# A decoder layer on one core: the decode step's delta rule with four heads on the partitions, its state products in column groups, and a new written-out order

## What is computed

```python
def gated_delta_rule(q, k, v, log_a, beta, s0):     # decode: one chunk of c = 4 tokens per sequence
    g = jnp.cumsum(log_a, axis=-1)
    decay = jnp.where(lower, jnp.exp(jnp.where(lower, diff, 0.0)), 0.0)     # diff = g_i - g_j
    kk = jnp.einsum("bhnid,bhnjd->bhnij", k, k)
    a_mat = eye + jnp.where(strict, beta[..., :, None] * kk * decay, 0.0)
    rhs = jnp.concatenate([v * beta[..., None], k * (beta * jnp.exp(g))[..., None]], axis=-1)
    sol = lax.linalg.triangular_solve(a_mat, rhs, left_side=True, lower=True, unit_diagonal=True)
    u, w = sol[..., :dv], sol[..., dv:]
    qk = jnp.einsum("bhnid,bhnjd->bhnij", q, k) * decay
    v_new = u_c - jnp.einsum("bhcd,bhde->bhce", w_c, s)
    o_c = (jnp.einsum("bhcd,bhde->bhce", q_c * jnp.exp(g_c)[..., None], s)
           + jnp.einsum("bhij,bhje->bhie", qk_c, v_new))
    s = (s * jnp.exp(g_last)[..., None]
         + jnp.einsum("bhcd,bhce->bhde", k_c * jnp.exp(g_last - g_c)[..., None], v_new))
```

## Time and profile before

| | us |
|---|---|
| runs | 1472.62, 1476.36, 1477.51 (median 1476.36) |
| the profiled execution's own time | 1477.91 |
| its span | 1476.1 |
| TensorE busy in the span | 1447.0 (98%) |
| VectorE, ScalarE, GpSimd busy | 712.0, 477.5, 204.0 |
| mean granted clock of TensorE | 0.988 |

### The profile page before, as it was taken

One profiled execution on the slowest core, in us unless ns is written; L12 is line 12 of the kernel. 1 busy time (PEld: TensorE's weight loads), 2 busy tenths in 40 slices (PEclk: granted clock), 3 DMA queues, 4 the chain that ended last, 5 costly groups with the idle time before them and its releaser, 6 DMA issues.

```text
span 1476.1 us, 25520 instructions
## 1 busy us (share of the span) xinstructions
PE 1447.0 (98%) x9772; PEld 1414.6 (96%) x9772; DVE 712.0 (48%) x1303; ACT 477.5 (32%) x876; POOL 204.0 (14%) x262
## 2 busy tenths in 40 slices
PE   7999999999999999999999999999999999999997
PEld 7899998999999899999999999999999999999997
DVE  5678844677663635433333333333333333344625
ACT  6324451442424424432130221302213022145525
POOL 3100213142243432000000000000000000140303
PEclk9999997999999999999999999999999999999999
DMA  7112421412223442211111111111111111112003
GB/s 181 44 44 58 101 77 30 131 59 65 80 77 77 96 88 56 55 46 44 43 44 55 45 43 43 43 53 48 43 43 44 50 51 43 43 43 73 30 29 118
DMA packets 166318, 89.88 MB, mean 61 GB/s; under 512 B 50763, under 2 KB 160267, under 8 KB 166230
## 3 DMA queue, kind: packets, MB, share of 16 engines
q1 hardware_dynamic: 165222, 84.89, 20.9%
q0 software_dynamic: 1008, 3.79, 0.6%
HBM read 77.97 MB, written 10.69 MB: 60 GB/s over the span
## 4 chain that ended last, share of the span: by engine, by line
PE 63%; DVE 2%; issue 1%; ACT 0%; DMA 0%; DVEq 0%; POOL 0%; SPq 0%
PE pg L712 62%; DVE act_lo L2040 1%; PE bk L1167 0%; DMA out<-y_tok 0%; DVE y_tok L2124 0%; PE bk L1097 0%; ACT act_hi L1186 0%; DVE xres L2164 0%; DVE tm L2161 0%; ACT sq L1186 0%; PE bk L1112 0%; ACT L1186 0%; DVE xres L2049 0%; PE bk L1158 0%; DVE tm L2150 0%
## 5 line engine op out<-in xcount | busy, mean ns | idle before, releaser
L712 PE MATMUL pg<-act_hi,w_hi 128*128 128x352 f32 x1320 | 428.9, 325 | 8.3 <-issue 3.7
L712 PE MATMUL pg<-act_lo,w_hi 128*128 128x352 f32 x1320 | 424.7, 322 | 0.0
L712 PE MATMUL pg<-act_hi,w_lo 128*128 128x352 f32 x1296 | 416.8, 322 | 0.0
L712 PEld LDWEIGHTS pg<-act_hi,w_hi 128*128 128x128 f32 x1320 | 249.0, 189 | 11.4 <-issue 5.9
L712 PEld LDWEIGHTS pg<-act_lo,w_hi 128*128 128x128 f32 x1320 | 249.5, 189 | 0.0
L712 PE MATMUL pg<-u_hi,w_hi 128*128 128x352 f32 x768 | 249.3, 325 | 0.0
L712 PE MATMUL pg<-u_hi,w_lo 128*128 128x352 f32 x768 | 248.9, 324 | 0.0
L712 PE MATMUL pg<-u_lo,w_hi 128*128 128x352 f32 x768 | 247.8, 323 | 0.0
L712 PEld LDWEIGHTS pg<-act_hi,w_lo 128*128 128x128 f32 x1296 | 244.1, 188 | 0.0
L1186 ACT ACTIVATE w_hi<-w_raw 128x1024 fp32r<-128x1024 f32 x111 | 117.0, 1054 | 354.5 <-PE pg L712 322.0
L2387 POOL TENSOR_TENSOR ssq<-ssq,sq 128x352 f32<-128x352 f32 x72 | 76.1, 1065 | 876.4 <-ACT sq L1186 875.5
(11 more groups left out here) (341 smaller groups left out, 1527.0 us busy)
## 6 DMA issues: line engine op xcount, KB each, us to landing
w_raw<-in_w_up SPq DMA_DIRECT2D x32, 512.0 KB, 4.0
w_raw<-in_w_down SPq DMA_DIRECT2D x32, 512.0 KB, 3.4
w_raw<-in_w_in SPq DMA_DIRECT2D x29, 512.0 KB, 3.8
x_tok<-in_x_prompt SPq DMA_DIRECT2D x8, 512.0 KB, 7.7
w_raw<-in_w_out SPq DMA_DIRECT2D x8, 512.0 KB, 4.3
x_col<-in_x_prompt SPq DMA_DIRECT2D x32, 128.0 KB, 2.7
w_raw<-in_w_ple_gate SPq DMA_DIRECT2D x8, 512.0 KB, 3.9
out<-y_tok SPq DMA_DIRECT2D x8, 512.0 KB, 3.0
```

What stands on the lines that cost most here:

```text
L712: last = mm(pg[bank][:, 0:TH], w, a, start=i == 0, stop=i == len(terms) - 1)
```

## The change

All four heads of the decode batch go on the partitions beside each other: the 4 x 32 = 128 (head, token) pairs are the rows of one 128x128 matrix, whose blocks off the diagonal are masked away (`m_smp`, `m_lev` are now 128x128, `m_bat` is 128x8, made from `m_row`). So each step is one product where it was four.

- `s_norm` also makes `q_col` (log decay, beta and the last factor as columns of 128 rows) by three products with one moving column; `s_begin` prepares them.
- `s_xt` is now a block transpose on VectorE and no step of TensorE; `s_turn` is gone; `s_kk` turns k and v.
- `s_in`: the k (steps 0, 1) and q (steps 2, 3) of a sequence, scaled and placed so that all other tokens are zero (`placed()`, in `pre[1]`, which GpSimd clears first), are 32 columns of weights, and the state is the moving operand with 128 columns. The products of the four heads go to four column groups (output partitions 0, 32, 64, 96) and accumulate over the 8 sequences. 64 products in all, 16 per step.
- `s_out` adds the q part by a product with the identity.
- `s_put 0` and `s_put 1`: four products each, one per head, with 32 rows (head h on rows 32h to 32h+31), 128 columns of weights and 512 moving columns, into four banks. GpSimd makes two copies of 128x512 instead of eight of 32x512. All four decays on VectorE come before the first add.
- The states are written out after the adds of `s_put 1`.
- `ORDER` is new for the whole mixer. The 1464 fills are the same; the new list has 157 steps, 89 of them with no fill behind them, the old one 168 and 69.

```diff
@@ ORDER, the stretch of the decode step @@
-z 0 6 25; kq 1 0 15; s_wait 0 0 10;
-s_begin 0 0 13; s_conv 0 0 14; s_norm 0 0 21; s_conv 1 0 7; s_kk 0 0 7; s_conv 2 0 10; s_xt 0 0 2; s_in 0 0 4;
-s_in 1 0 4; s_y 0 0 2; s_in 2 0 4; s_in 3 0 3; s_z 0 0 2; s_in 4 0 4; s_in 5 0 4; s_in 6 0 4; s_in 7 0 4;
-s_turn 0 0 7; s_solve 0 0 10; s_out 0 0 14; s_onorm 0 0 0; s_put 0 0 0; s_put 1 0 11; s_put 2 0 0;
-s_put 3 0 14; s_put 4 0 0; s_put 5 0 23; s_put 6 0 0; s_put 7 0 52; diff 2 0 0; vturn 0 0 0; vturn 1 0 0;
-diff 3 0 18; kk 2 0 0; into 0 0 0; kk 3 0 6; kturn 0 0 2; solve 0 0 15; b1 2 0 0; b2 2 0 67; b3 2 0 0;
+z 0 6 75; kq 1 0 0; s_wait 0 0 0;
+s_begin 0 0 0; s_conv 0 0 44; s_norm 0 0 1; s_conv 1 0 30; s_kk 0 0 0; s_conv 2 0 8; s_in 0 0 3; s_xt 0 0 0;
+s_in 1 0 2; s_y 0 0 8; s_in 2 0 3; s_in 3 0 2; s_z 0 0 4; s_solve 0 0 12; s_out 0 0 13; s_onorm 0 0 0;
+s_put 0 0 27; s_put 1 0 67; vturn 0 0 0; diff 2 0 0; vturn 1 0 0; diff 3 0 30; kk 2 0 0; into 0 0 0; kk 3 0 0;
+kturn 0 0 17; solve 0 0 19; b1 2 0 20; update 0 0 0; sum 0 0 0; b2 2 0 11; b3 2 0 60; b4 2 0 5; into 1 0 0;
...
@@ names @@
+        QSQ, QN, YC, GAM = [LY[0][:, i, :] for i in range(4)]
+        KSQ, KN, PTB, OSQ = [LY[1][:, i, :] for i in range(4)]
+        DEC, AMAT, LOWB, XTB = [AT[1][:, i, :] for i in range(4)]
+        VT, U, KT, WV = [XT1[0][:, i, :] for i in range(4)]
+        PUT_BANKS = (bk[0], bk[2], bk[3], bk[4])
+        PUT = (AT[0], X[0])
+        def zone(b, i):
+            return bk[b][:, P * i:P * i + P]
+        def by_head():
+            return pre[1][:, PAD:PAD + TP].rearrange("p (h i m) -> p h i m", h=H, m=TS)
+        def placed():
+            pitch = pre[1][:, :].ap[0][0]
+            return bass.AP(pre[1], PAD, [[pitch, P], [TS * NB, H], [TS + NT, NB], [1, NT]])
@@ SyncE @@
-                        sp.wait_ge(sm.s_out_made, 2 * (h + 1))
+                        sp.wait_ge(sm.s_out_made, H + h + 1)
@@ TensorE @@
-            def against_state(g):
-                for i in range(4 * g, 4 * g + 4):
-                    last = mm(bk[4][:, 8 * i:8 * i + 8], S_in[:, i // NB, i % NB, :], F0[:, 8 * i:8 * i + 8], start=True, stop=True)
+            def against_state(c, i0):
+                for i in range(i0, i0 + NB // 2):
+                    for h in range(H):
+                        last = mm(zone(4, c)[quad(h)], by_head()[:, h, i, :], S_in[:, h, i, :], start=i % NB == 0, stop=i == NB - 1)
...
                 elif k == "s_norm":
+                    for j in range(3):
+                        last = mm(bk[3][:, j:j + 1], X0[:, j, :], ones[0:TS, 0:1], start=True, stop=True)
...
                 elif k == "s_kk":
+                    mm(zone(0, 1), KN, KN, start=True, stop=True)
+                    mm(zone(0, 2), KN, QN, start=True, stop=True)
+                    turn(zone(3, 0), KN, ident[:, :])
+                    turn(zone(3, 1), WV, ident[:, :]).then_inc(sm.q_pe, 1)
...
                 elif k == "s_in":
-                    last = against_state(c)
+                    elif c == 2:
+                        pe.wait_ge(sm.q_dve, 12)
+                    last = against_state(c // 2, c % 2 * (NB // 2))
...
+                elif k == "s_out":
+                    mm(zone(1, 0), WV, PTB, start=True, stop=False)
+                    mm(zone(1, 0), QSQ, ident[:, :], start=False, stop=True).then_inc(sm.q_pe, 1)
...
                 elif k == "s_put":
-                    if c >= 4:
-                        pe.wait_ge(sm.s_out_made, c - 3)
-                    mm(bk[c % 4][:, :], F0[0:TS, c // 2 * P:(c // 2 + 1) * P], by_seq[c % 4][0:TS, :, :],
-                       start=True, stop=True).then_inc(sm.q_pe, 1)
+                    pe.wait_ge(sm.q_pool, 6 + c)
+                    if c == 0:
+                        pe.wait_ge(sm.q_act, 13)
+                        pe.wait_ge(sm.q_dve, 14)
+                    else:
+                        pe.wait_ge(sm.s_out_made, H)
                     for h in range(H):
+                        last = mm(PUT_BANKS[h][:, :], KT[quad(h)], PUT[c][quad(h), :, :], start=True, stop=True)
@@ VectorE @@
+                elif k == "s_xt":
+                    dve.wait_ge(sm.q_pool, 5)
+                    nc.vector.transpose(XB, XTB).then_inc(sm.q_dve, 1)
...
                 elif k == "s_put":
-                    dve.wait_ge(sm.q_pe, 10 + c)
-                    dve.wait_ge(sm.q_dve, 13 + c // 2)
-                    part = S_in[:, c // 2, 4 * (c % 2):4 * (c % 2) + 4, :]
-                    tt(part, part, heads(bk[c % 4]), ADD).then_inc(sm.s_out_made, 1)
+                    dve.wait_ge(sm.q_pe, 9 + c)
+                    dve.wait_ge(sm.q_dve, 18)
+                    dve.wait_ge(sm.states_out, 16 * 6)
+                    for h in range(H):
+                        now = S_in[:, h, 4 * c:4 * c + 4, :]
+                        tt(now, now, heads(PUT_BANKS[h]), ADD).then_inc(sm.s_out_made, 1)
@@ GpSimd @@
                 elif k == "s_begin":
+                    nc.gpsimd.memset(pre[1][:, PAD:PAD + TP], 0.0).then_inc(sm.q_pool, 1)
...
+                elif k == "s_out":
+                    for i in range(2):
+                        tt(PUT[i][:, :, :], WV[:, None, :].to_broadcast([P, 4, P]), spread(m_bat[:, 4 * i:4 * i + 4], P), MUL) \
+                            .then_inc(sm.q_pool, 1)
```

More of the change, by code:

```diff
@@ L66 @@
[L66 to L74, removed]
+begin 0 0 0; diff 0 0 8; diff 1 0 1; kk 0 0 90; kk 1 0 21; b1 0 0 3; b2 0 0 72; b3 0 0 9; b4 0 0 58; y 0 4 0;
@@ new lines @@
+y 2 4 0; y 3 4 0; norm 0 0 0; z 2 4 0; z 3 4 0; kturn 1 0 12; y 2 5 0; kq 2 0 0; solve 1 0 10; update 1 0 0;
+z 2 5 0; sum 1 0 0; kq 3 0 0; y 2 6 20; z 2 6 0; norm 1 0 0; scale 0 0 0; diff 4 0 0; scale 1 0 7; vturn 2 0 0;
+vturn 3 0 0; diff 5 0 39; kk 4 0 22; kk 5 0 0; into 2 0 11; kturn 2 0 0; b1 4 0 37; solve 2 0 0; b2 4 0 16;
+update 2 0 0; b3 4 0 0; sum 2 0 17; b4 4 0 43; into 3 0 0; y 4 4 0; y 5 4 0; norm 2 0 21; kturn 3 0 0; z 4 4 0;
+z 5 4 0; solve 3 0 0; y 4 5 0; kq 4 0 0; update 3 0 5; z 4 5 0; sum 3 0 0; y 4 6 20; z 4 6 0; norm 3 0 0;
@@ new lines @@
+scale 2 0 0; kq 5 0 0; scale 3 0 17; vturn 4 0 0; vturn 5 0 0; diff 6 0 0; kturn 4 0 0; diff 7 0 26; kk 6 0 0;
+kk 7 0 0; into 4 0 47; b1 6 0 23; solve 4 0 0; b2 6 0 0; b3 6 0 29; update 4 0 0; b4 6 0 0; sum 4 0 45;
+into 5 0 0; kq 6 0 1; y 6 4 8; y 7 4 0; norm 4 0 32; kturn 5 0 0; z 6 4 0; z 7 4 0; solve 5 0 11; update 5 0 0;
+y 6 5 0; kq 7 0 6; z 6 5 0; sum 5 0 0; y 6 6 18; z 6 6 0; norm 5 0 0; scale 4 0 9; scale 5 0 0; vturn 6 0 8;
+vturn 7 0 0; into 6 0 0; kturn 6 0 11; solve 6 0 6; update 6 0 0; sum 6 0 0; kturn 7 0 18; into 7 0 0;
@@ L75 @@
+norm 6 0 10; solve 7 0 26; update 7 0 0; sum 7 0 0; scale 6 0 37; norm 7 0 0; scale 7 0 0; tail 0 0 0
 """
@@ new lines, in _ @@
+                    pe.wait_ge(sm.q_dve, 10)
+                    mm(zone(1, 1), LOWB, XB, start=True, stop=True).then_inc(sm.q_pe, 1)
+                elif k == "s_z":
+                    pe.wait_ge(sm.q_act, 12)
+                    mm(zone(1, 2), YC, XTB, start=True, stop=True).then_inc(sm.q_pe, 1)
+                elif k == "s_solve":
+                    pe.wait_ge(sm.q_dve, 13)
+                    mm(zone(2, 2), XTB, U, start=True, stop=True).then_inc(sm.q_pe, 1)
+                elif k == "s_out":
[3 more added lines that the diff above has]
+                    mm(zone(1, 0), QSQ, ident[:, :], start=False, stop=True).then_inc(sm.q_pe, 1)
+                elif k == "s_onorm":
+                    pe.wait_ge(sm.q_act, 14)
+                    mm(zone(1, 1), ones[:, :], OSQ, start=True, stop=True).then_inc(sm.q_onorm, 1)
+                elif k == "s_put":
+                    pe.wait_ge(sm.q_pool, 6 + c)
+                    if c == 0:
+                        pe.wait_ge(sm.q_act, 13)
+                        pe.wait_ge(sm.q_dve, 14)
+                    else:
+                        pe.wait_ge(sm.s_out_made, H)
@@ L1973, in _ @@
                 elif k == "s_norm":
                     dve.wait_ge(sm.q_pe, 1)
+                    nc.vector.tensor_copy(q_col[:, :], bk[3][:, 0:3]).then_inc(sm.q_dve, 1)
+                    dve.wait_ge(sm.q_dve, 4)
                     dve.wait_ge(sm.q_act, 7)
-                    for h in range(H):
-                        ts_(F2[0:TS, h * TS:(h + 1) * TS], bk[2][0:TS, h * TS:(h + 1) * TS], g_tok[0:TS, NTT, h:h + 1],
-                            0.0, SUB, MIN).then_inc(sm.q_diff, 1)
-                    dve.wait_ge(sm.q_act, 6)
@@ L2223, in _ @@
                 put_state(b)
-            for dst in (m_inc[:, :], m_smp[:, :], m_blk[:, :], m_bat[:, :]):
+            for dst in (m_inc[:, :], m_smp[:, :], m_blk[:, :], m_row[:, :]):
                 nc.gpsimd.memset(dst, 1.0).then_inc(sm.made, 1)
```

250 lines of the change are left out of this document (88 added, 162 removed).

## The result

| | us |
|---|---|
| before, 4 runs on the same chip | median 1474.49 (1470.92 to 1477.51) |
| after, 4 runs | median 1450.40 (1449.72 to 1451.63) |
| ratio | 0.9832, 95% interval 0.9802 to 0.9862 |
| the profiled execution after | 1451.63, span 1449.9, mean clock 0.996 |

The change made the kernel 24 us faster. The forecast was 17 us and its range ended at 1452, 1.6 us above the result. The direction and the mechanism were right, and more was won than the range allowed.

The account below looks back on a forecast made before the run. TensorE, busy 98% of the span, was taken as the bound. 1476.4 - 10.0 (small products) - 8.0 (clock) - 0.5 (idle) - 0.7 (joined steps) + 1.5 (new waits) = 1458.7, say 1459 us; range 1452 to 1470.

Parts of the forecast that it names:

- Rest of the small products: Decode-stage products on TensorE other than `s_in` and `s_put`: 3.9 us instead of 6.8, 2.9 saved.
- `s_in`: Its 128 records on four column groups, three out of four overlapping: 5.4 us, a saving of 1.7; bounds 4.4 and 14.7.
- The rival that they take turns: Groups in `s_in` and `s_put` run one after another: 14.7 and 7.6 us, kernel 1473 with the clock holding; chance 0.10.
- its extreme, 1494: Column groups at `s_in` take turns, every weight load is paid, and the clock falls: 1494 us; chance 0.05.
- `s_put`: Its 16 records of 512 columns on four row groups: 3.0 us, a saving of 5.4; bounds 2.5 and 7.6.
- The clock: TensorE's granted clock, at 0.50 for 17 us in the decode stage, would hold at 1.00: 8.0 us back.
- falls again: Rival: the granted clock drops in the new decode stage too, 1467 us; chance 0.14.
- The idle time at `s_put`: TensorE's 0.5 us wait there would go, with two masked GpSimd copies instead of four before the first product: -0.5 us.
- the balance that I feared there: VectorE's decays and adds before `s_put 1`, 10.2 us, just fit TensorE's 10.5; part of a new-waits rival, 1467, chance 0.12.
- The last two terms: In the new order: 1.5 us allowed for new waits, and -0.7 us for joined steps of 16, 32 and 64 rows.
- more is won: Rival: clock falls such as the 3.3 us one at 501 us may go, groups fully parallel: 1452 us; chance 0.03.

Follow-up runs that it names:

- The kernel with the heads outside: The kernel after with the loops of `s_in` turned round, head in the outer loop and sequence inside, same 64 products; 1456.66 us.
- the wide kernel: The kernel before with the `s_in` products moving 128 columns each instead of 8, same weights and records; 1468.98 us, and 1468.06 when run again.
- the wide kernel with the new order: The kernel before with 128 moving columns at `s_in` and, outside its old decode step, the order of the kernel after; 1464.79 us.
- the last set: The third set of experiment runs, with 23 runs of the unchanged kernel before, median 1473.07 us, and the kernel after again at 1450.20.

## Why the prediction fell short

- **Rest of the small products: right.** 3.7 us, 3.9 forecast.
- **`s_in`: mechanism right, size off.** The size that was off is "I take three out of four" column groups. All four ran at once: 4.8 us instead of 5.4, near the bound of 4.4 below. The kernel with the heads outside shows what the order of the groups brings, 6.3 us. The rival that they take turns (1473) is refuted, and with it its extreme, 1494.
- **`s_put`: the same.** 2.3 us instead of 3.0, at the bound of 2.5 below. I had rounded both kinds away from the ends; together 1.3 us too little.
- **The clock: right in the pair of profiles, half right in the runs.** It held at 1.00 (rival "falls again", 1467, refuted), and it gave back 8.0 us where it had fallen. But the earlier trace rows are one execution; 32 of 54 are of the kind with the lower mean clock, and taking the fall away is worth 4.8 and 5.0 us between the medians (1473.77 to 1468.98 and 1473.07 to 1468.06; the intervals of both ratios end just below 1, at 0.9996 and 0.9999, so the size of this term is known only roughly). The cause that I argued, few moving columns, is shown by the wide kernel; what more fills between would do stays open.
- **The idle time at `s_put`: right**, and the balance that I feared there held. The four adds behind `s_put 0` were over at 227.5 us and `s_put 1` began at 228.04. The decays and adds took what the earlier trace rows said:

```profile
L2012 DVE TENSOR_TENSOR S_in<-S_in,LY 128x1024 f32<-128x1024 f32 x4 | 6.3, 1636 | 0.0
L2023 DVE TENSOR_TENSOR S_in<-S_in,bk 128x512 f32<-128x512 f32 x8 | 4.9, 678 | 1.3 <-PE bk L1066 1.3
```

- **The last two terms: wrong, and this is the step that failed.** "I allow 1.5 us of new waits" measured 0.2, and "-0.7" for the joined steps was mis-sized: the two together were to be +0.8 and are -3.2 between the profiles, and 2.6 to 3.3 us of gain in the runs. The price was right, 0.4 us for going to a small shape and back; the count was wrong. -0.7 is less than two of them, and the new list has seven pairs of like steps joined that stood apart before, 2.8 us. The kernel with the joins split shows 0.4 us at each of the seven and nothing at its other 28 places.
- **What was not in the sum**: falls of the clock outside `s_in`, at the start-up (3.4 us in the first profiles) and at `s_put` (4.7 us in the wide kernel with the new order, a shorter one in the second profile of before). They explain the remainder only in part: from that kernel's 1464.8 to after's 1450.2 are 14.6 us, of which products and idle are 11.8. Of its 12 runs the six fastest, at a mean clock of 0.994 to 0.998, lie 13.1 above after (median 1463.3 against 1450.2). So 1.3 us are left, and for the other 1.5 the fall at `s_put` is likely, but of this kernel there is one profile. That profile and the second one of after differ by 17.7 us: 16.8 in the stage with the fills taken out, 4.7 of them the fall and 12.0 products and idle (the wide kernel's 49.5 less 29.8 and 48 fills give the same 12.0, where the earlier trace rows gave 11.8), 0.5 at the start-up, 0.6 behind the mixer, and 0.2 less in the mixer behind the stage. Profiles of one kernel differ by more than that at the start-up and behind the mixer.

By the runs' medians, then: products and idle 11.8, clock at `s_in` 5.0, order 3.3, 20.1 together; against 10.5, 8.0 and a loss of 0.8 in the forecast. The rest to 24.1 is the 2.8 just told and 1.2 by which the medians differ between the first four runs and the last set (1473.07 to 1474.49 for before, less after's own 0.2). That the forecast came as close as 8 us is in part luck: it rests on a clock term that was 3 too large. And the range was too narrow below: with "more is won" at 0.03 it ended at 1452, although the bounds below of `s_in` and `s_put` (1.5 us together), waits at nothing (1.5) and seven joins at 0.4 (2.1 more than mine) already added up to 1453.6, and falls like the one at 500 us in the earlier trace rows could go as well as come.

By the strict reading of "TensorE: Matmul & The Clock Gate" of the Trainium skill, Part 3, The mechanism, an `s_in` step would cost 4.6 us (an estimate: the 18.2 of the prediction over four). The timeline has 1.2, with all four row groups in use in every product, so its weight loads were hidden although the row group never differs. That different tiles load weights and multiply in parallel, as "TensorEngine Tiling (Array Packing)" of the Trainium skill, Key Properties, says, is what the trace shows. The factors of 2.38 and 3.07 that "TensorE: Matmul & The Clock Gate" of the Trainium skill, Part 3, reports for three column and four row tiles are here 3.4 (32 records of 0.107 against 1.01) and 3.2 (8 of 0.427 against 1.07) for four, entry included.

## What to carry to other kernels

Put products whose column groups differ directly behind each other, with the group in the innermost loop: the same 64 products cost 4.8 us that way and 10.4 with the groups in the outer loop. Four row groups at 512 columns a product gained as much. Count the places where TensorE goes to a small shape and back between large products as a cost of their own, invisible in busy time and waits: here 0.4 us each. Two steps of the same small shape directly behind each other save one of them; joining steps of unlike shape saved nothing. Before a fall of the clock in one profile goes into a sum at its full length, look at whether the runs fall into two kinds: here three executions out of five were of the slower one.

## What the chip showed that I had not expected

- The clock fell with TensorE busy without a gap: 128x128 float32 weights against 8 columns, 8 records a step, a step every 1.5 to 2.4 us with fills between. The same steps with 128 columns took the same time (0.81 us) and left the clock at 1.00, so more work cost less.
- How long it stayed down differed: 17 us in the first profile of before, 13.7 in the second, which then fell once more at `s_put`, for 3.4; the stage was as long in both (57.3 and 57.4 us).
- 32 records of 128 columns on four column groups took 1.01 us, 0.03 each; the weight loads of 32 columns, of all rows, were hidden.
- 128 columns at a time on a row group, four times before the next group (0.09 us a record in `s_put` in pieces), use the groups far worse than 512 at a time (0.13 us a record of four times the columns).
